# A two-layer hybrid trunk on one core: feature-major input and output, halved first weights, one sum product per norm, and named activation tables

## What is computed

```python
def rmsnorm(x, gain):
    y = xf * lax.rsqrt(jnp.mean(xf * xf, axis=-1, keepdims=True) + NORM_EPS)
    return (y * gain.astype(jnp.float32)).astype(x.dtype)
def swiglu(h, w_gate, w_up, w_down):
    return (jax.nn.silu(h @ w_gate) * (h @ w_up)) @ w_down
def reference(...):
    for layer in range(DEPTH):
        x = x + 0.5 * swiglu(rmsnorm(x, norm_gain[layer, 0]), ...)
        h = rmsnorm(x, norm_gain[layer, 1])
        x = x + (conv_sparse_attn_mixer(h, ...) if layer % 2 == 0 else gated_deltanet_mixer(h, ...))
        x = x + 0.5 * swiglu(rmsnorm(x, norm_gain[layer, 2]), ...)
    return rmsnorm(x, final_gain)
```

## Time and profile before

| | |
|---|---|
| median of 3 runs | 2305.44 us (2303.66 to 2305.83) |
| span of the profiled execution | 2302.4 us |
| TensorE: busy share, mean granted clock | 98%, 0.995 |
| VectorE, ScalarE, GpSimd busy | 49%, 42%, 10% |
| moved by DMA | 185.9 MB, 81 GB/s |

### The profile page before, as it was taken

The page is one execution under the profiler, slowest core; times in us unless marked ns, Lnnn a source line. Parts: engine busy times, 40 slices in busy tenths (PEclk is TensorE's granted clock), DMA queues, the critical chain, the costliest instruction groups (busy, mean ns, idle before and its releaser), DMA issues.

```text
span 2302.4 us, 27083 instructions
## 1 busy us (share of the span) xinstructions
PE 2248.3 (98%) x10326; PEld 1783.7 (77%) x10326; DVE 1127.4 (49%) x1607; ACT 971.2 (42%) x1195; POOL 233.5 (10%) x155
## 2 busy tenths in 40 slices
PE   6999999999999999999999999899999999999998
PEld 5888888656667888888788888678888877888886
DVE  4444444587734444423444432477777554444423
ACT  4444322224544443322444322557667554444222
POOL 1000000123111000000000000033332300000000
PEclk9999999999999999999999999999999999999999
DMA  4332322212112233322233322211111122322321
GB/s 144 96 91 92 111 101 64 81 55 65 47 55 92 91 93 98 109 95 79 85 98 92 98 103 91 65 46 37 38 37 38 38 82 86 97 91 91 118 89 50
DMA packets 48560, 185.90 MB, mean 81 GB/s; under 512 B 6368, under 2 KB 6496, under 8 KB 48480
## 3 DMA queue, kind: packets, MB, share of 16 engines
q1 hardware_dynamic: 48480, 184.80, 25.4%
HBM read 182.68 MB, written 2.10 MB: 80 GB/s over the span
## 4 chain that ended last, share of the span: by engine, by line
PE 91%; DVE 4%; ACT 2%; issue 1%; POOL 0%; DMA 0%; ACTq 0%; SPq 0%; DVEq 0%; POOLq 0%
PE prod L408 27%; PE prod L410 26%; PE prod L409 26%; PE misc L617 4%; PE misc L550 1%; PE prod L507 1%; PE misc L568 1%; DVE qc L1364 1%; PE misc L668 1%; PE misc L640 1%; DVE qc L1362 0%; PE misc L530 0%; ACT w_hi L758 0%; PE misc L559 0%; POOL sq_acc L1405 0%
## 5 line engine op out<-in xcount | busy, mean ns | idle before, releaser
L992 DVE TENSOR_TENSOR w_lo<-raw,w_hi 128x1024 fp32r<-128x1024 f32 (+1 forms) x301 | 405.1, 1346 | 814.6 <-ACT w_hi L758 814.6
L408 PE MATMUL prod<-h_hi,w_hi 128*128 128x512 f32 x1904 | 793.4, 417 | 8.3 <-DVE h_lo L998 5.0
L410 PE MATMUL prod<-h_hi,w_lo 128*128 128x512 f32 x1904 | 754.3, 396 | 0.0
L409 PE MATMUL prod<-h_lo,w_hi 128*128 128x512 f32 x1904 | 754.2, 396 | 0.0
L758 ACT ACTIVATE w_hi<-raw 128x1024 fp32r<-128x1024 f32 (+1 forms) x318 | 356.8, 1122 | 574.7 <-PE prod L410 574.2
L408 PEld LDWEIGHTS prod<-h_hi,w_hi 128*128 128x128 f32 x1904 | 359.8, 189 | 125.5 <-issue 47.3
L410 PEld LDWEIGHTS prod<-h_hi,w_lo 128*128 128x128 f32 x1904 | 358.8, 188 | 86.2
L409 PEld LDWEIGHTS prod<-h_lo,w_hi 128*128 128x128 f32 x1904 | 359.5, 189 | 83.5 <-issue 10.4
L410 PE MATMUL prod<-a_hi,w_lo 128*128 128x512 f32 x704 | 278.8, 396 | 0.0
L409 PE MATMUL prod<-a_lo,w_hi 128*128 128x512 f32 x704 | 278.1, 395 | 0.0
L408 PE MATMUL prod<-a_hi,w_hi 128*128 128x512 f32 x704 | 277.6, 394 | 0.0
(11 more groups left out here) (235 smaller groups left out, 2131.9 us busy)
## 6 DMA issues: line engine op xcount, KB each, us to landing
raw<-in_w SPq DMA_DIRECT2D x254, 512.0 KB, 3.6
raw<-in_wd SPq DMA_DIRECT2D x64, 704.0 KB, 4.0
x_rows<-in_x SPq DMA_DIRECT2D x1, 2048.0 KB, 7.8
out<-y_rows SPq DMA_DIRECT2D x4, 512.0 KB, 4.0
consts<-in_consts SPq DMA_DIRECT2D x1, 832.0 KB, 10.8
hf<-in_pos SPq DMA_DIRECT2D x1, 256.0 KB, 11.5
consts<-in_consts SPq DMA_DIRECT2D x1, 64.0 KB, 1.8
od_conv<-in_od_conv SPq DMA_DIRECT2D x1, 48.0 KB, 3.0
```

Of the source, the lines that this page charges most:

```text
L408: pe.matmul(bank, wh, hi, start=first and k == 0, stop=False)
L409: pe.matmul(bank, wh, lo, start=False, stop=False)
L410: ins = pe.matmul(bank, wl, hi, start=False, stop=last and k == tiles_n - 1)
L992: dve.tensor_tensor(w_lo[:, n % 2, 0:w], raw[:, n % 4, 0:w], w_hi[:, n % 2, 0:w].bitcast(F32), ALU.subtract).then_inc(lo_ready, 1)
```

## The change

- SP transfers x feature-major in eight pieces straight into `x`, with the first unit's weights in two halves between the first pieces; gains and eps are issued by ACT. The transposes and copies at the start are gone. Constants come later.
- `first_unit` (the unit right behind a norm) runs w_hi h_hi and w_lo h_hi for all eight tiles first, then w_hi h_lo. At the start it begins with the first half of the weights.
- POOL adds seven pairs in place of six (`ACCS`), so one product with ones gives the sum. It stands behind the second unit in an FFN, and three matmuls into the second unit in a mixer.
- ACT loads the table set that has Ln and Exp by name ahead of the last tile, and the silu set behind a norm; the first pass of the FFN loop is written out, with the split of unit n0+2 ahead of the norm. The same split moves ahead of the norm at both mixers.
- The result stays feature-major: DVE scales six tiles and POOL two (`y_out`), and SP stores eight pieces. The host turns it over.

```diff
-            sp.dma_start(const["ident"], A["consts"][:, 0, :]).then_inc(setup_in, 16)
-            sp.dma_start(x_rows[:], A["x"].rearrange("(t p) d -> p t d", p=P)).then_inc(setup_in, 16)
-            sp.dma_start(gains[:], A["gains"]).then_inc(setup_in, 16)
-            sp.dma_start(eps[:], A["eps"]).then_inc(setup_in, 16)
-            for u in range(4):
-                load(u, A["w8"][GU_ROW[0] + u])
-                if u == 1:
-                    sp.dma_start(consts[:, 1:, :], A["consts"][:, 1:, :]).then_inc(consts_in, 16)
+            sp.dma_start(x[:, 0, :], A["x"][:, 0, :]).then_inc(x_in[0], 16)
+            sp.dma_start(raw[:, 0, 0:HALF0], A["w8"][GU_ROW[0]][:, 0:HALF0]).then_inc(half_in, 16)
+            sp.dma_start(x[:, 1, :], A["x"][:, 1, :]).then_inc(x_in[1], 16)
+            sp.dma_start(raw[:, 0, HALF0:KT * P], A["w8"][GU_ROW[0]][:, HALF0:KT * P]).then_inc(raw_in[0], 16)
+            for k in range(2, KT):
+                sp.dma_start(x[:, k, :], A["x"][:, k, :]).then_inc(x_in[k], 16)
+            load(1, A["w8"][GU_ROW[0] + 1])
+            sp.dma_start(consts[:], A["consts"]).then_inc(consts_in, 16)
+            load(2, A["w8"][GU_ROW[0] + 2])
+            load(3, A["w8"][GU_ROW[0] + 3])
...
-            for i in range(TT // 2):
-                for t, scaled in ((i, y_scaled_v), (TT // 2 + i, y_scaled_s)):
-                    sp.wait_ge(scaled, i + 1)
-                    sp.dma_start(out[t * P:(t + 1) * P, :], y_rows[:, t, :]).then_inc(stored, 16)
-            sp.wait_ge(stored, 16 * TT)
+            for m, scaled, count in STORES:
+                sp.wait_ge({"v": y_scaled_v, "p": y_scaled_p}[scaled], count)
+                sp.dma_start(out[m * P:(m + 1) * P, :], y_out[:, m, :]).then_inc(stored, 16)
+            sp.wait_ge(stored, 16 * KT)
...
-                pe.wait_ge(acc_done, 6 * (r + 1))
-                pe.matmul(misc[:, 0, :], const["ones"], sq_acc[:], start=True, stop=False)
-                pe.wait_ge(sq_ready, 8 * (r + 1))
-                pe.matmul(misc[:, 0, :], const["ones"], sq[:, 1, :], start=False, stop=True).then_inc(sum_done, 1)
+                pe.wait_ge(acc_done, ACCS * (r + 1))
+                pe.matmul(misc[:, 0, :], const["ones"], sq_acc[:], start=True, stop=True).then_inc(sum_done, 1)
 
             def first_unit(r, n, bank):
 
-                unit(n, bank, 0, h_act, True, True, wait_k=lambda k: pe.wait_ge(h_ready, 8 * r + k + 1),
-                     between=lambda k: square_sum(r) if k == KT - 1 else None)
-
-            def turn_y(m):
-
-                pe.wait_ge(y_made, m + 1)
-                if m >= 3:
-                    pe.wait_ge(y_rows_in, m - 2)
-                ins.then_inc(y_turned, 1)
+                for k in range(KT):
+                    if n == 0 and k == 0:
+                        pe.wait_ge(half_lo, 1)
+                    elif k == (0 if n else KT // 2):
+                        pe.wait_ge(lo_ready, n + 1)
+                    pe.wait_ge(hhi_ready, 8 * r + k + 1)
+                    pe.matmul(bank, w_hi[:, n % 2, k * P:(k + 1) * P], h_hi[:, k, :], start=k == 0, stop=False)
+                    pe.matmul(bank, w_lo[:, n % 2, k * P:(k + 1) * P], h_hi[:, k, :], start=False, stop=False)
+                for k in range(KT):
+                    pe.wait_ge(h_ready, 8 * r + k + 1)
+                    ins = pe.matmul(bank, w_hi[:, n % 2, k * P:(k + 1) * P], h_lo[:, k, :], start=False,
+                                    stop=k == KT - 1)
+                ins.then_inc(unit_done, 1)
...
+                        if first and u == 2:
+                            square_sum(norm_of(f))
...
-                        if f == NFFN - 1 and m >= 2 and half == 1:
-                            turn_y(m - 2)
...
-            pe.wait_ge(setup_in, 16 * SETUP)
-            for k in range(KT):
-                if k >= 4:
-                    pe.wait_ge(x_in, k - 3)
-                for t in range(TT):
-                    ins = pe.transpose(prod[:, k % 4, t * P:(t + 1) * P], x_rows[:, t, k * P:(k + 1) * P], const["ident"])
-                ins.then_inc(x_turned, 1)
-            pe.wait_ge(x_in, KT)
...
+                    if u == 1 and k == 0:
+                        square_sum(1)
...
-            turn_y(KT - 2)
-            for t in range(TT):
-                a = slice(t * P, (t + 1) * P)
-                pe.wait_ge(acc_done, 6 * 7)
-                pe.matmul(misc[:, 0, t:t + 1], sq_acc[:, a], const["ones"][:, 0:1], start=True, stop=False)
-                pe.wait_ge(sq_ready, 8 * 7)
-                ins = pe.matmul(misc[:, 0, t:t + 1], sq[:, 1, a], const["ones"][:, 0:1], start=False, stop=True)
-            ins.then_inc(sum_done, 1)
-            turn_y(KT - 1)
+            pe.wait_ge(acc_done, ACCS * 7 - 1)
+            pe.matmul(misc[:, 0, :], const["ones"], sq_acc[:], start=True, stop=False)
+            pe.wait_ge(sq_ready, 8 * 7)
+            pe.matmul(misc[:, 0, :], const["ones"], sq[:, 1, :], start=False, stop=True).then_inc(sum_done, 1)
...
-                    act.activation(warm[:], eps[:], ACT.Ln)
+                    act.preload_act_table_set(LN_EXP)
...
-                with act.Fori(0, FT // 2 - 1) as i:
+                split(n0 + 2)
+                norm(norm_of(f))
+                act.preload_act_table_set(SILU)
+                pair(0, peeled=True)
+                with act.Fori(1, FT // 2 - 1) as i:
...
-            act.wait_ge(setup_in, 16 * SETUP)
+            act.dma_start(gains[:], A["gains"]).then_inc(gains_in, 16)
+            act.dma_start(eps[:], A["eps"]).then_inc(gains_in, 16)
+            act.preload_act_table_set(LN_EXP)
+            act.wait_ge(gains_in, 16 * 2)
             for k in range(KT):
-                act.wait_ge(x_in, k + 1)
+                act.wait_ge(x_in[k], 16)
                 hi(0, k)
-                if k in (0, 1):
-                    split(k)
+                if k < 2:
+                    a = slice(k * HALF0, (k + 1) * HALF0)
+                    act.wait_ge((half_in, raw_in[0])[k], 16)
+                    act.activation(w_hi[:, 0, a], raw[:, 0, a], ACT.Copy).then_inc((half_hi, hi_ready)[k], 1)
+                if k == KT - 1:
+                    split(1)
             for k in range(KT):
                 square(0, k)
-            norm(0)
             ffn_act(0)
+            split(EV_N + 2)
...
-            norm(5)
             ffn_act(3)
-            act.wait_ge(sum_done, 7)
-            link(act.activation(rstd_row[:], misc[:, 0, 0:TT], ACT.Ln, bias=eps[:], scale=1.0 / D))
-            act.activation(rstd_row[:], rstd_row[:], ACT.Exp, scale=-0.5).then_inc(rstd_ready, 1)
-            act.wait_ge(rstd_ready, 7)
-            act.wait_ge(y_rows_in, KT)
-            for t in range(TT // 2, TT):
-                act.activation(y_rows[:, t, :], y_rows[:, t, :], ACT.Copy, scale=rstd_row[:, t:t + 1]).then_inc(y_scaled_s, 1)
+            norm(6)
...
-            for k in range(KT):
-                dve.wait_ge(x_turned, k + 1)
-                dve.tensor_copy(x[:, k, :], prod[:, k % 4, :]).then_inc(x_in, 1)
-                if k >= 6:
-                    split(k - 6)
+            for k in range(2):
+                a = slice(k * HALF0, (k + 1) * HALF0)
+                dve.wait_ge((half_hi, hi_ready)[k], 1)
+                ins = dve.tensor_tensor(w_lo[:, 0, a], raw[:, 0, a], w_hi[:, 0, a].bitcast(F32), ALU.subtract)
+                ins.then_inc((half_lo, lo_ready)[k], 1)
             for k in range(KT):
                 lo(0, k)
+            split(1)
             ffn_dve(0)
 
...
-            for m in range(KT - 3, KT):
-                rows(m)
-            dve.wait_ge(y_rows_in, KT)
             dve.wait_ge(rstd_ready, 7)
-            for t in range(TT // 2):
-                dve.tensor_scalar(y_rows[:, t, :], y_rows[:, t, :], rstd_row[:, t:t + 1], None, ALU.mult)\
-                    .then_inc(y_scaled_v, 1)
+            dve.wait_ge(y_made, KT)
+            for m in V_STORES:
+                dve.tensor_tensor(y_out[:, m, :], y_feat[:, m, :], rstd[:], ALU.mult).then_inc(y_scaled_v, 1)
 
...
-                for m in range(1, 7):
+                for m in range(1, KT - (r == 6)):
...
+            pool.wait_ge(rstd_ready, 7)
+            pool.wait_ge(y_made, KT)
+            for m in P_STORES:
+                pool.tensor_tensor(y_out[:, m, :], y_feat[:, m, :], rstd[:], ALU.mult).then_inc(y_scaled_p, 1)
```

More of the change, by code:

```diff
@@ L150, in delta_slots @@
     return out
+LN_EXP, SILU = "natural_log_exp_and_others", "silu_and_others"
+ACCS = KT - 1
+HALF0 = KT * P // 2
+P_STORES = (2, 5)
+V_STORES = tuple(m for m in range(KT) if m not in P_STORES)
+STORES = [(0, "v", 1), (1, "v", 2), (2, "p", 1), (3, "v", 3), (4, "v", 4), (6, "v", 5), (5, "p", 2), (7, "v", 6)]
 TU = 2 * LEVELS - 1
@@ L227, in __call__ @@
                 return t
-        io = Plan()
-        x_rows = io("x_rows", [TT, D])
         ffn = Plan()
@@ L287, in tiles @@
             return ap.rearrange("p (t c) -> p t c", t=TT)
```

(33 more changed lines are left out.)

19 lines of the change are left out of this document (5 added, 14 removed).

## The result

The changed kernel takes 2253.45 us (median of 4 runs, 2251.98 to 2254.17) against 2304.99 before: a ratio of 0.9774, interval 0.976 to 0.9788. That is 51.5 us less where 21 were forecast, and outside the range of 2278 to 2290. The direction was right, the size was not, and the 30 us beyond the forecast were not in any term of the sum.

A forecast was written before the change was run, and what follows sets the result against it. PE was taken to bound the kernel, so only its idle places could give time. Start 16.4, later FFNs 2.4, mixers 1.0 and end 1.3 sum to 21.1 less: 2305.4 to 2284; range 2278 to 2290.

The forecast's parts named there:

- Everything else I leave where it is: Opening analysis: apart from the waits named, nothing changes; feed-forward stretches run gapless at 232.6 or 227.3 ns a matmul, difference unexplained.
- a rival with 0.14: Second matrices of the second, third and last FFN take the quicker known pace: 2277 to 2281, chance 0.14.
- The start: First FFN: fourth unit starts at 30.8 instead of 47.16, set by POOL's additions: 16.4 us less.
- the transfers keep up: At the start: x and two units at 413 GB/s take 7.5 us, second unit there at about 9.8.
- The later FFNs: Three later FFNs: new h_hi wait 0.75, one product fewer 0.86, third-unit wait 1.03 gone, fourth-unit wait 0.30: 2.4 us less.
- The table drain: Rival: each table load also drains, holding silu 1.28 longer at four places, 5.1 us in all: 2289.1, chance 0.04.
- The mixers: Both mixers: rstd about 0.6 earlier as one table load goes; attention gives at most 0.4; 1.0 us less together.
- The end: Last stretch without transposes 1.0 us less, behind the last matmul 0.3 less.
- the loss of pace that the prediction allowed for: Last stretch: without transposes it may keep the slower pace, 5.3 ns on some 400 matmuls, 2.1 us.
- late gains: Rival at the start: gains and eps land at 9 behind x, everything 5.3 us later: 2289.3, chance 0.12.
- Slower than before: Rival: with gaps gone, all 6,336 FFN matmuls run slower, 33.6 us: 2318, chance 0.03.
- The last sign of being wrong: Listed sign against the forecast: 80 us FFN stretches with matmul counts other than 344 and 352.

The follow-up runs named there:

- x1: Changed kernel with an unused 16-byte tile (32 as allocated) put back where rstd_row stood, so all tiles from raw on lie 32 bytes higher; 2285.48 us.
- x6_all64: Changed kernel with an unused 64-byte tile ahead of x, so all tiles move alike by 64 bytes; 2250.74 us.
- x10: Changed kernel with the first unit behind a norm in its old order everywhere but at the start; 2247.16 us.
- x12: Changed kernel with stage tiles 192 bytes higher, third unit ahead of the start's sum, old first-unit order elsewhere, all last products on DVE; 2237.88 us.
- x11: Changed kernel with all eight last products on DVE, none on POOL; 2251.51 us.
- x13: Changed kernel with w_lo alone 32 bytes higher, all other tiles keeping their place modulo 256; 2283.89 us.
- x4: Changed kernel with only w_hi and w_lo 32 bytes higher, all else keeping its place modulo 64; 2289.90 us.

## Where the prediction was right and wrong

**The step that failed** stands in its first part: "Everything else I leave where it is." The pace of the matmuls was seen (344 against 352 in the earlier trace rows) and called unexplained, and a change of it was carried as a rival with 0.14 and a reach of 2277. It covered only the second matrices, at the 5.3 ns between two known rows; a pace quicker than both rows, in the gate and up units too, was not thought of. The rows were also read too quick: a window counts matmuls that only reach into it, 350 and 343 start in those 80 us, and from start to start the two paces are 228.9 and 233.3, 4.4 ns apart. The gate and up units gave 6.6 to 6.7 us in each of four FFNs (229.60 to 223.04 in the first; 248.33 to 241.64 between x1 and after). The cause lay in the change: a tile of 16 bytes that vanished ahead of the weights. With that tile put back the median is 2285.48, where 2284 was forecast. That it comes so near is in part luck: the terms below were not all met, and in x1's profile, of the slowest of its four runs, the span is 14.0 shorter than before (2302.4 to 2288.3), with 13.5 at the start.

**The start** was to bring the fourth unit to 30.8; it came at 34.76, so 12.4 us were gained in place of 16.4. Gains and eps landed at 5.06 and not 3.7 (eps took 3.9 from its issue, not 3.2), and the second unit's weights only at 13.1, after ACT was through with h_hi, where 9.8 was forecast. That "the transfers keep up" was wrong: 413 GB/s were taken from about 2.2 on, and the windows of after show 248 from 2 to 6 us and 363 from 6 to 10. The first square came at 14.10 and POOL's first addition at 15.32 in place of 12.4. POOL's additions went at 1.34 each (8.06/6), near the 1.30 taken. The mis-sized terms are these landings, 2.2 us at the sum, and the clock: the sum was put at the lower level, the third unit was not. That is the other 1.8, since PE and not the chain over Ln, Exp and silu then set the fourth unit. How long the lower level lasts differs between runs: in the windows of x6_all64 full clock is back at 28.0, where after has it at 31.4.

```profile
28.00:31.20 3.20, 3.20 (x15) 2.61 (x15) 0.69 (x1) 3.17 (x4) 0.00 (x0) 1.00 0.31 119
```

**The later FFNs** were right in each part: a new wait for the last h_hi of 0.7 to 0.8 (the matmul at 699.12 comes 1.02 behind the one ahead of it, 0.79 over the pace), one product in place of two, no wait at the third unit, and one ahead of the fourth (713.58, 0.50 behind the last, 0.27 over the pace, where 0.30 was forecast). With the pace of before, the stage went from 249.18 to 248.33: 0.85 less, and 0.84 was the sum. x10 shows that the first of these parts was a loss that could be had back.

**The table drain** did not occur. In the timeline of after, at the second FFN, the load starts 0.02 behind the end of Exp (708.74 + 0.63) and silu 0.02 behind the load, so the rule of the Trainium skill (ScalarE: Activation LUTs, section What ACT_TABLE_LOAD costs) is not borne out where a load is issued ahead:

```profile
709.39 1.28 ACT L786 ACT_TABLE_LOAD   x1
...
710.69 0.63 ACT L782 ACTIVATE silu_g<-silu_g 128x512 f32<-128x512 f32 x1
```

**The mixers**: 1.0 less together was forecast. The attention mixer took 0.62 less with the old pace (270.36 to 269.74 in x1, without its output matrix). The other took 0.4 more with its output matrix (455.03 to 455.43); it varies by more than that between runs (452.84 in x10, 456.91 in x12).

**The end**: 1.3 less in all was forecast. In x1 the last second matrix and the end took 0.74 less (137.30 to 136.56). The stretch without transposes is the gain, 1.1 (124.1 to 123.0, first matmul to last): its products went at 233.3, and between the transposes they had gone at 229.7, which is the loss of pace that the prediction allowed for. In after, at 228.9, it took 120.6. Behind the last matmul of the second matrix it became 13.6 us from 13.2, where 0.3 less was forecast, since POOL's two products held DVE up (1.25 less without them in x11).

Of the rivals, late gains was partly so (5.06, not 9). Slower than before named the right term, the pace in all FFNs, with the wrong sign and another reason: it went by gaps between matmuls, where the runs show the places of the tiles. The last sign of being wrong, FFN stretches with other counts, came true.

## What to carry over

When a diff adds or drops a tile, compare the offsets of everything that is allocated behind it: here 16 bytes (32 as allocated) were worth more than all the reordering. In a stretch that is bound by PE, as these FFNs are, try moving tiles and weights at the same offset modulo 256 bytes, and check the pace from start to start where nothing else bounds it. And look for idle PE ahead of a late dependency: here work moved into it saved 6.8 us, and the clock stayed up behind it.

## What the hardware did that was not expected

- The pace of matmuls with 128x512 in float32 depends on the distance of the moving tile to the weights in SBUF, modulo 256 bytes: 226.7 ns at 0, 228.9 or 233.3 at 64, 232.4 to 233.3 at the others tried, at full granted clock. In the gate and up units the mean is the same 233.3 when w_lo alone is 32 off (x13) as when w_hi and w_lo are (x4).
- The same wait of PE is followed by a stretch at the lower level in one run and not in another. Behind 2.28 us from one matmul's start to the next in the delta-rule mixer's output matrix the windows of after show a granted clock of 0.52 from 1836.9 on; x11_tail, with the same 2.28, shows 1.00 there (1837 to 1840). The output matrix took 47.73 and 46.13.

```profile
1836.90:1840.00 3.10, 3.10 (x9) 2.40 (x8) 1.83 (x2) 1.14 (x2) 0.00 (x0) 0.52 0.00 0
```
